# Which expert pairs return their rows through DRAM, and when those rows are read back

## The chip, the cores and the metric

The kernel runs on one core of a Trainium2 chip. The metric is the device time of one launch in microseconds. Its TensorE (PE) does matrix products, VectorE (DVE), ScalarE (ACT) and GpSimd (POOL) do the rest, and SyncE (SP) issues most of the transfers. All engines run their own instruction streams and wait for one another on semaphores.

## What is computed

Two layers of a decoder step over 288 tokens (256 of a new sequence and 8 x 4 of running ones), width 1024. A layer mixes (RG-LRU, a convolution group, retention) and then applies a mixture of experts; this case is about the second half:

```python
g_sel = argmax(softmax(x @ wg + bg))                 # one of 4 groups
top_v, top_i = top_k(logits of that group, 2)         # 2 of its 8 experts
gates = p_group * softmax(top_v)
for e in range(32):                                   # every expert
    h = silu(x @ w1[e]) * (x @ w3[e])                 # 1024 -> 256
    y += gates[:, e] * (h @ w2[e])                    # 256 -> 1024
x = x + y
```

The kernel gathers for each expert the tokens that chose it (up to 64 slots), so 288 x 2 = 576 of the 2048 slots hold a token.

## The kernel before

The 32 experts of a layer are worked off in 16 pairs, two experts of 64 slots each making 128 rows. Their weights stream from DRAM: w1, w3 and w2 of an expert are 1 MB each, and a ring in SBUF holds four experts. SP issues w1 and w3 of an expert when the products of the expert four before it have been made (it waits on bank "h"), and w2 when the products of an earlier pair's w2 are done (bank "y1"). The weights of two experts stay outside the ring: expert 6 (EARLY, in pair 3) and expert 16 (SPARE, in pair 8), whose w1 and w3 lie in `uT` and `mixT`. SP's queue is one list of transfers, in the order in which the weights are used.

For each pair PE does `up` for the even expert (32 matmuls with w1 and w3, line 1135), `down` for the pair before (16 matmuls with w2, line 1158), the transposes of hidden rows and of the next pair's tokens, and `up` for the odd expert. ACT copies each `up` out of PSUM (lines 2201, 2223, one copy for each expert), scales the results of `down` by the gates into `ysb` (`results`, line 2196), and does the tanh. DVE does the gating product (`hidden`) and the evacuation of the tokens. POOL gathers the rows of pair g + 3 by an indirect DMA.

The results of a pair, 128 rows in slot order, go back to the tokens in one of two ways:

- **By DRAM**, pairs 0 to 5 (`VIA_DRAM = 6`): POOL scatters `ysb` to `y_scratch` (`scatter`, line 2344). ACT may write the next `ysb` when the scatter has landed. Later `read_back` (line 2363) fetches for each token of a tile of 128, 128 or 32 tokens its one or two rows (two indirect DMAs), into two buffers `again[0]` and `again[1]` that `clear` has set to zero, and DVE adds both to `x` (`sums`, line 1919). The three tiles share the two buffers, so this happens in three rounds: POOL reads tile 1 at pair 6, tile 2 at pair 9, tile 0 at pair 11, and DVE adds at pairs 9, 11 and 13 (`READ_BACK`).
- **By matmul**, pairs 6 to 15: POOL makes a 0/1 matrix from the token numbers (`way_back`, line 2353), DVE splits `ysb` into three bf16 parts (`rest`, `low`), and PE multiplies (`give_back`, lines 1172, 1181, 1187). Parts 0 and 1 of pair p come at the end of pair p + 1, parts 2, 3 and 4 after the even `up` of pair p + 2. DVE adds the five banks to `x` (`given_back`).

PE's list for one pair of the second kind is:

```python
up(2 * pair, it)
if p - 2 >= VIA_DRAM:
    give_back(p - 2, (2, 3))
    give_back(p - 2, (4,))
down(1 - pair, it if pair else it - 1)
...
up(2 * pair + 1, it)
...
if p - 1 >= VIA_DRAM:
    give_back(p - 1, (0, 1))
```

Of the kernel before, what the change touches and what calls it, by code (L numbers as in the profile page):

```python
# [46 lines left out]
NPAIR = NE // 2  # L47
VIA_DRAM = 6
BY_MATMUL = NPAIR - VIA_DRAM
READ_BACK = {VIA_DRAM + 3: 1, VIA_DRAM + 5: 2, VIA_DRAM + 7: 0}  # L50

# [112 lines left out]
def x1_turn(pair):  # L164

    return pair + max(0, pair - VIA_DRAM - 2)


def back_plan():

    plan = {}
    for p in range(VIA_DRAM, NPAIR):
        for a, b in enumerate((6, 7, 6, 7, 1) if p < NPAIR - 2 else (6, 7, 0, 1, 6) if p < NPAIR - 1 else (3, 7, 0, 1, 2)):
            plan[p, a] = b, x1_turn(p + 3) - 1 if p < NPAIR - 2 and a == 4 else PER_BANK[b] - EXPERT_BASE[b]
            PER_BANK[b] += 1
    return plan
# [25 lines left out]
def build(nc, ins, outs):  # L202
# [11 lines left out]
    with ExitStack() as ctx:  # L214
# [132 lines left out]


        again = [ttf, sgf[:, 512:512 + D]]
        assert used <= 512  # L350
        spare_w1 = uT[:, 0:2048].rearrange("p (k f) -> p k f", k=KT)
        spare_w3 = mixT[:, :, :].rearrange("p k t -> p (k t)")[:, 0:2048].rearrange("p (k f) -> p k f", k=KT)
        spare_w2 = [a[:, :, :].rearrange("p a n -> p (a n)")[:, 0:D] for a in (qT, kr)]

        glsf = gls[:, :, :, :].rearrange("p c b t -> p (c b t)")
# [365 lines left out]
        def _(pe):  # L721
# [54 lines left out]
            for l in range(DEPTH):  # L776
# [385 lines left out]
                def give_back(p, parts):  # L1162

                    pair, it = pair_of(p)
                    turn_ = l * BY_MATMUL + p - VIA_DRAM
                    if 0 in parts:
                        pe.wait_ge(back_ready, turn_ + 1)
                    if 4 in parts:
                        b = begin("back4", pair, it)
                        for n_, y in enumerate((y_top, y_mid, y_low)):  # L1170
                            for q in range(4):
                                i = pe.matmul(b[32 * q:32 * q + 32, 0:256], back[:, pair, SEQ:NT], y[:, 256 * q:256 * q + 256],  # L1172
                                              start=n_ == 0, stop=n_ == 2, skip_group_check=True)
                        finish(i, "back4", pair, it)
                        return
                    banks = []
                    for a in parts:
# [12 lines left out]

                def give_back_last():

                    pe.wait_ge(back_ready, BY_MATMUL * (l + 1))
                    for a in range(4):
# [20 lines left out]
                def experts2_back(p):  # L1215

                    pair, it = pair_of(p)
                    up(2 * pair, it)
                    if p - 2 >= VIA_DRAM:
                        give_back(p - 2, (2, 3))  # L1220
                        give_back(p - 2, (4,))
# [5 lines left out]
                    if p + 1 < NPAIR:  # L1227
                        tokens(pair + 1, it, (1,))
                        turn_h(2 * pair + 1, it)
                    if p - 1 >= VIA_DRAM:  # L1230
                        give_back(p - 1, (0, 1))
# [10 lines left out]
                experts2(1, 0)  # L1242
                for it in range(1, VIA_DRAM // 2):
                    experts2(0, it)
                    experts2(1, it)
                for p in range(VIA_DRAM, NPAIR):
                    experts2_back(p)
# [53 lines left out]
        def _(dve):  # L1301
# [87 lines left out]
            for l in range(DEPTH):  # L1389
# [425 lines left out]
                def overs():  # L1815

                    do(dve.tensor_copy(r_if[:, :, :], r_idx[:, :, 0:2]))
                    own(S(again_here[:, :, :], r_if[:, :, :], float(2 * VIA_DRAM), None, ALU.is_lt))
                    do(S(again_rank[:, :, :], rank[:, :, :], float(SLOTS), None, ALU.is_lt))
# [71 lines left out]
                def rest(p, j):  # L1891

                    pair, it = pair_of(p)
                    if j == 0 and p > VIA_DRAM:
                        xfull(dve, "back4", *pair_of(p - 1), l)
                    xfreed(dve, f"y{j}", pair, it, l)
                    T(y_rest[:, halves[j]], ysb[:, halves[j]], y_top[:, halves[j]], ALU.subtract).then_inc(rest_ready, 1)  # L1897

                def low(p):
                    turn_ = l * (BY_MATMUL - 1) + p - VIA_DRAM  # L1900
                    for j, s in enumerate(halves):
# [3 lines left out]
                def clear():  # L1905

                    own(dve.memset(again[0], 0.0))
                    own(dve.memset(again[1], 0.0))
                    own.wait()
                    dve.sem_inc(again_clear, 1)  # L1910

                def sums(p, t):
# [5 lines left out]
                    for k in range(2):  # L1918
                        T(x[0:n, t, :], x[0:n, t, :], again[k][0:n, :], ALU.add).then_inc(sums_added, 1)
                        dve.wait_ge(sums_added, 6 * l + 2 * list(READ_BACK).index(p) + k + 1)  # L1920

# [21 lines left out]
                def experts2_back(p):  # L1943
                    pair, it = pair_of(p)
                    if p - 2 >= VIA_DRAM:
                        given_back(p - 2, (0, 1))
                        if p in READ_BACK:
                            sums(p, READ_BACK[p])
                        given_back(p - 2, (2, 3, 4))
                    if p - 1 >= VIA_DRAM:  # L1950
                        rest(p - 1, 0)
                    hidden(2 * pair, it)
                    if p - 1 >= VIA_DRAM:
                        rest(p - 1, 1)
                        low(p - 1)
                    if p + 1 < NPAIR:
                        tokens(pair + 1, it)
                    hidden(2 * pair + 1, it)
                    if p in READ_BACK and p + 2 in READ_BACK:
                        clear()  # L1960

# [6 lines left out]
                experts2(1, 0)  # L1968
                with dve.Fori(1, VIA_DRAM // 2) as it:
                    experts2(0, it)  # L1970
                    experts2(1, it)
                clear()
                for p in range(VIA_DRAM, NPAIR):
                    experts2_back(p)
# [49 lines left out]
        def _(act):  # L2024
# [27 lines left out]
            for l in range(DEPTH):  # L2052
# [145 lines left out]
                def one(u, it, first=False):  # L2198
# [3 lines left out]
                    if u % 2 == 0 and not first:  # L2202
                        before = (1 - u // 2, it if u else it - 1)

                        act.wait_ge(scattered, 16 * (l * VIA_DRAM + 2 * before[1] + before[0]))
                        results(*before)
# [10 lines left out]
                def one_back(p, i):  # L2217
# [6 lines left out]
                    if i == 0:  # L2224
                        xfull(act, "back4", *pair_of(p - 2), l)
                        results(*pair_of(p - 1))
# [13 lines left out]
                one(3, 0)  # L2240
                with act.Fori(1, VIA_DRAM // 2 + 1) as it:
                    for u in range(4):
                        one(u, it)
                for p in range(VIA_DRAM + 2, NPAIR):
                    for i in range(2):
                        one_back(p, i)
# [25 lines left out]
        def _(pool):  # L2272
# [3 lines left out]
            for l in range(DEPTH):  # L2276
# [71 lines left out]
                def way_back(g):  # L2348

                    if g - 2 >= VIA_DRAM:  # L2350
                        xfull(pool, "back4", *pair_of(g - 2), l)
                    for t, (o, n) in enumerate(TILES):
# [3 lines left out]
                def read_back(t):  # L2356

                    o, n = TILES[t]
                    pool.wait_ge(again_ready, l + 1)
                    pool.wait_ge(scattered, 16 * VIA_DRAM * (l + 1))  # L2360
                    pool.wait_ge(again_clear, 3 * l + list(READ_BACK.values()).index(t) + 1)
                    for k in range(2):
                        pool.indirect_dma_start(out=again[k][0:n, :], out_offset=None, in_=y_dram,
                                                in_offset=bass.IndirectOffsetOnAxis(ap=again_at[0:n, t, k:k + 1], axis=0),
# [9 lines left out]
                for g in range(NPAIR):  # L2374
                    if g + 3 < NPAIR:
                        gather(g + 3)
                    if g < VIA_DRAM:
                        scatter(g)
                    else:
                        way_back(g)  # L2380
                    if g in (VIA_DRAM + 3, VIA_DRAM + 5):
                        read_back(READ_BACK[g + 2])
                    if g + 2 < NPAIR:
                        if g >= VIA_DRAM:
# [3 lines left out]
                    if g == VIA_DRAM:  # L2388
                        read_back(READ_BACK[g + 3])
                o = O[l]  # L2390
# [36 lines left out]
```

## Time and profile before

| | |
|---|---|
| time, median of 3 runs | 856.33 us (855.98 to 857.28) |
| the profiled execution, its own time | 856.64 us |
| its span | 854.8 us |
| PE busy | 817.4 us, 96% of the span |
| DVE / ACT / POOL busy | 480.7 / 176.1 / 145.6 us |
| moved from and to DRAM | 260.12 MB, mean 304 GB/s |
| pairs 0 to 15 of layer 0 / of layer 1 on PE | about 184 to 429 us / 605 to 846 us |

Times in the profile are microseconds from the span's start. The profiled execution takes 1.8 us more than its span. The page gives shares over the whole span; the expert part has to be read from windows and from the order in time.

### The profile page before, as it was taken

What the parts mean: (1) busy time and instruction counts of PE and PEld (TensorE: products, weight loads), DVE (VectorE), ACT (ScalarE), POOL (GpSimd) and SP (SyncE); (2) the same over time, 40 slices, a digit from 0 to 9 for tenths busy, and PEclk for the clock granted to TensorE, in tenths of its full rate; (3) what the DMA queues carried; (4) which work ended last, traced back from release to release, by engine and by line L of the source; (5) the groups of instructions that cost most, each with busy time, mean ns of one, the idle gap of its engine ahead of it and who ended that gap; (6) DMA issues with size and microseconds to landing.
All of it is one profiled execution on the core that took longest, in us unless ns stands there. A gap on an engine that the chain in (4) does not pass through costs nothing.

```text
span 854.8 us, 13483 instructions
## 1 busy us (share of the span) xinstructions
PE 817.4 (96%) x5250; PEld 462.8 (54%) x5250; DVE 480.7 (56%) x1097; ACT 176.1 (21%) x361; POOL 145.6 (17%) x197
## 2 busy tenths in 40 slices
PE   7999999999997899999999999999999979999995
PEld 5664554675654555555466545447655545545552
DVE  3497787372212377775555977955521215777666
ACT  3213122302121111111221221232022111111113
POOL 0030031011211322321000300300211112412220
PEclk9999999999999999999999999999999999999998
DMA  9942962779999999999960339357799999999961
GB/s 320 318 156 104 375 208 74 274 257 405 417 414 382 413 415 403 415 414 400 374 247 0 148 138 257 102 140 268 307 411 414 416 413 417 413 401 415 414 257 57
DMA packets 89946, 260.12 MB, mean 304 GB/s; under 512 B 30424, under 2 KB 40044, under 8 KB 73946
## 3 DMA queue, kind: packets, MB, share of 16 engines
q1 hardware_dynamic: 80410, 247.01, 75.5%
q0 software_dynamic: 7680, 9.39, 3.2%
q10 hardware_dynamic: 1792, 2.84, 0.9%
q8 instruction: 44, 0.72, 0.4%
q14 instruction: 20, 0.16, 0.1%
HBM read 265.22 MB, written 15.18 MB: 328 GB/s over the span
## 4 chain that ended last, share of the span: by engine, by line
PE 89%; DVE 4%; issue 3%; DMA 2%; SPq 1%; ACT 1%; DVEq 0%; POOLq 0%; ACTq 0%
PE psum L1135 27%; PE psum L1158 13%; PE psum L793 12%; PE psum L733 8%; PE psum L802 7%; PE psum L991 5%; PE psum L1187 4%; PE psum L1181 2%; PE psum L812 2%; DMA ring<-in_w_in 1%; PE psum L1032 1%; PE psum L1172 1%; PE psum L868 1%; PE psum L1022 1%; PE psum L893 1%
## 5 line engine op out<-in xcount | busy, mean ns | idle before, releaser
L1135 PE MATMUL psum<-ring,arena 128*64 128x256 f32 x1920 | 222.1, 384 | 9.2 <-issue 8.0
L1135 PEld LDWEIGHTS psum<-ring,arena 128*64 128x64 f32 x1920 | 138.3, 138 | 78.7 <-issue 19.1
L1158 PE MATMUL psum<-ring,arena 128*64 128x512 f32 x480 | 116.4, 597 | 7.6 <-issue 7.6
L793 PE MATMUL psum<-ring,uT 128*128 128x512 f32 x256 | 113.6, 596 | 0.5 <-DVE uT L1369 0.4
L1877 DVE TENSOR_TENSOR arena<-psum,gff 128x512 f32<-128x512 f32 x64 | 43.6, 687 | 69.3 <-PE psum L733 69.3
L1885 DVE SCALAR_TENSOR_TENSOR arena<-arena,psum 128x128 f32<-128x128 f32 x64 | 18.3, 285 | 108.4 <-ACT arena L2215 94.8
L793 PEld LDWEIGHTS psum<-ring,uT 128*128 128x128 f32 x256 | 47.6, 190 | 55.1 <-issue 53.2
L1931 DVE TENSOR_TENSOR x<-x,psum 128x512 f32<-128x512 f32 x80 | 51.4, 683 | 40.9 <-PE psum L1187 35.3
L2196 ACT ACTIVATE arena<-psum,sg 128x512 f32<-128x512 f32 x64 | 44.0, 687 | 121.9 <-PE psum L1158 120.1
L1158 PEld LDWEIGHTS psum<-ring,arena 128*64 128x64 f32 x480 | 35.3, 137 | 61.2 <-issue 60.1
L2331 POOL DMA_INDIRECT rows<-xn_scratch,sg x32 | 33.5, 1047 | 204.1 <-PE psum L733 119.2
L802 PE MATMUL psum<-uT,ring 128*128 128x288 f32 x256 | 63.8, 407 | 0.7 <-DMA ring<-in_w_in 0.7
L1456 DVE SCALAR_TENSOR_TENSOR cb<-glp,prm,cb 128x256 f32<-128x256 f32 x120 | 57.3, 546 | 0.6 <-DVE hst L1608 0.4
L991 PE MATMUL psum<-ring,mixT 128*128 128x512 f32 x128 | 57.2, 597 | 0.0
L802 PEld LDWEIGHTS psum<-uT,ring 128*128 128x128 f32 x256 | 48.1, 190 | 14.7 <-DMA ring<-in_w_in 1.2
L733 PE MATMUL psum<-const,rows 128*128 128x128 f32 (+1 forms) x304 | 48.7, 289 | 0.5 <-DMA rows<-xn_scratch,sg 0.3
L733 PEld LDWEIGHTS psum<-const,rows 128*128 128x128 f32 (+1 forms) x304 | 39.5, 193 | 14.7 <-issue 12.8
L2353 POOL TENSOR_SCALAR kT<-const,sg 128x128 bf16<-128x128 f32 (+3 forms) x60 | 41.8, 711 | 17.8 <-PE psum L1172 17.2
L1897 DVE TENSOR_TENSOR v<-arena 128x512 f32<-128x512 f32 x36 | 24.8, 688 | 27.6 <-ACT arena L2196 27.6
L2201 ACT ACTIVATE arena<-psum 128x256 f32<-128x256 f32 x30 | 11.5, 383 | 136.9 <-PE psum L1135 136.9
L2223 ACT ACTIVATE arena<-psum 128x256 f32<-128x256 f32 x32 | 12.3, 383 | 129.9 <-PE psum L1135 129.9
L991 PEld LDWEIGHTS psum<-ring,mixT 128*128 128x128 f32 x128 | 23.7, 190 | 27.0 <-issue 26.6
(330 smaller groups left out, 938.1 us busy)
## 6 DMA issues: line engine op xcount, KB each, us to landing
ring<-in_moe_w SPq DMA_DIRECT2D x180, 1024.0 KB, 19.2
ring<-in_w_in SPq DMA_DIRECT2D x24, 1024.0 KB, 14.0
ring<-in_w_out SPq DMA_DIRECT2D x8, 1024.0 KB, 7.2
y_scratch<-in_w_out SPq DMA_DIRECT2D x1, 2304.0 KB, 17.9
arena<-in_state_ret SPq DMA_DIRECT2D x16, 128.0 KB, 5.6
out<-arena SPq DMA_DIRECT2D x16, 128.0 KB, 2.5
xn_scratch<-rows ACTq DMA_DIRECT2D x4, 512.0 KB, 4.0
mixT<-in_moe_w SPq DMA_DIRECT2D x2, 1024.0 KB, 4.9
```

What stands on the lines that cost most here:

```text
L733: return pe.transpose(out, in_, ident[0:n, 0:n])
L793: i = pe.matmul(b, uTk[:, k, 128 * t:128 * t + 128], w[:, k, :], start=k == 0, stop=k == KT - 1)
L802: i = pe.matmul(b, w[:, k, 128 * (c % 4):128 * (c % 4) + 128], uTk[:, k, :], start=k == 0, stop=k == KT - 1)
L991: i = pe.matmul(b, mixT[:, k, 128 * t:128 * t + 128], w[:, :, k, :], start=k == 0, stop=k == 3, skip_group_check=True)
L1135: i = pe.matmul(b[64 * j:64 * j + 64, 0:FE], xsT[:, u // 2, k, s], weight13(e, j, k), start=k == 0, stop=k == KT - 1, skip_group_check=True)
L1158: i = pe.matmul(b[64 * q:64 * q + 64, :], hT[:, q, f, :], weight2(4 * it + 2 * pair + q, f, j), start=f == 0, stop=f == 1, skip_group_chec ...
L1187: i = pe.matmul(b, back[:, pair, 64 * (a - a % 2):64 * (a - a % 2) + 128], y[:, 512 * (a % 2):512 * (a % 2) + 512], start=False, stop=y is ...
L1456: chain[c] = own(STT(dst, glp[:, c, k:k + SEQ], w, dst, ALU.mult, ALU.add))
L1877: T(xsT[:, g2 % 2, k0:k0 + 4, :], psum[:, b, :].rearrange("p (k s) -> p k s", k=4), g3[:, k0:k0 + 4, :], ALU.mult).then_inc(bank_free[b], 1)
L1931: i = T(s, s, psum[:, b, :], ALU.add)
L2196: A(ysb[:, 512 * j:512 * j + 512], psum[:, b, :], ACT.Copy, scale=gate_col[:, pair:pair + 1]).then_inc(bank_free[b], 1)
L2353: i = pool.tensor_scalar(back[:, g % 2, o:o + n] if g < NPAIR - 1 else back_last[:, o:o + n], C("iota")[:, 0:n], tok[:, t, g:g + 1], None, ...
```

## The change

Pairs 0 to 3 and 8 and 9 go by DRAM, pairs 4 to 7 and 10 to 15 by matmul: six and ten as before. The three tiles have two buffers each (`mixT` for tile 0, the old two for tile 1, `uT` for tile 2), all cleared at once ahead of pair 10; POOL issues the six read-backs one after the other after pair 11, and DVE adds at pairs 13 (tile 1), 14 (tile 2) and 15 (tile 0). The test of which expert numbers go by DRAM has two more DVE operations in each layer. The loops of the first pairs are shorter, and pairs 4 and 5 are written out with the rest.

```diff
-VIA_DRAM = 6
-BY_MATMUL = NPAIR - VIA_DRAM
-READ_BACK = {VIA_DRAM + 3: 1, VIA_DRAM + 5: 2, VIA_DRAM + 7: 0}
+
+FIRST = 4
+VIA_DRAM = (*range(FIRST), 8, 9)
+BY_MATMUL = [p for p in range(NPAIR) if p not in VIA_DRAM]
+READ_BACK = {13: 1, 14: 2, 15: 0}
...
-    return pair + max(0, pair - VIA_DRAM - 2)
+    return pair + sum(p <= min(pair, NPAIR) - 3 for p in BY_MATMUL)
...
-        again = [ttf, sgf[:, 512:512 + D]]
...
+        mixTf = mixT[:, :, :].rearrange("p k t -> p (k t)")
+        again = [[mixTf[:, 0:D], mixTf[:, D:2 * D]], [ttf, sgf[:, 512:512 + D]], [uT[:, 0:D], uT[:, D:2 * D]]]
...
-                    if p - 2 >= VIA_DRAM:
+                    if p - 2 in BY_MATMUL:
                         give_back(p - 2, (2, 3))
                         give_back(p - 2, (4,))
...
-                    if p - 1 >= VIA_DRAM:
+                    if p - 1 in BY_MATMUL:
                         give_back(p - 1, (0, 1))
...
-                    own(S(again_here[:, :, :], r_if[:, :, :], float(2 * VIA_DRAM), None, ALU.is_lt))
+
+                    lo, hi = 2 * VIA_DRAM[FIRST], 2 * VIA_DRAM[-1] + 1
+                    do(S(again_here[:, :, :], r_if[:, :, :], float(lo), None, ALU.is_ge))
+                    do(STT(again_here[:, :, :], r_if[:, :, :], float(hi), again_here[:, :, :], ALU.is_le, ALU.mult))
+                    do(STT(again_here[:, :, :], r_if[:, :, :], float(2 * FIRST), again_here[:, :, :], ALU.is_lt, ALU.add))
...
-                    own(dve.memset(again[0], 0.0))
-                    own(dve.memset(again[1], 0.0))
+                    for t, (_, n) in enumerate(TILES):
+                        for k in range(2):
+                            own(dve.memset(again[t][k][0:n, :], 0.0))
...
-                clear()
-                for p in range(VIA_DRAM, NPAIR):
+                for p in range(FIRST, NPAIR):
+                    if p == VIA_DRAM[-1] + 1:
+                        clear()
                     experts2_back(p)
...
                     if i == 0:
-                        xfull(act, "back4", *pair_of(p - 2), l)
+                        if p - 2 in VIA_DRAM:
+                            act.wait_ge(scattered, 16 * (l * len(VIA_DRAM) + VIA_DRAM.index(p - 2) + 1))
+                        else:
+                            xfull(act, "back4", *pair_of(p - 2), l)
                         results(*pair_of(p - 1))
...
-                    if g < VIA_DRAM:
+                    if g in VIA_DRAM:
                         scatter(g)
                     else:
                         way_back(g)
-                    if g in (VIA_DRAM + 3, VIA_DRAM + 5):
-                        read_back(READ_BACK[g + 2])
+                    if g == VIA_DRAM[-1] + 2:
+                        for t in READ_BACK.values():
+                            read_back(t)
```

## Rows read from the trace of the kernel before

**Rows 1.** The page, the span in 40 slices of 21.4 us: DMA share, rate.

```profile
DMA  9942962779999999999960339357799999999961
GB/s 320 318 156 104 375 208 74 274 257 405 417 414 382 413 415 403 415 414 400 374 247 0 148 138 257 102 140 268 307 411 414 416 413 417 413 401 415 414 257 57
```

**Rows 2.** Busy time by windows: PE, PEld, DVE, ACT, POOL, clock, DMA share, GB/s.

```profile
206.00:222.00 16.00, 16.00 (x126) 9.37 (x124) 3.57 (x9) 3.25 (x8) 3.31 (x4) 1.00 1.02 417
...
270.00:286.00 16.00, 13.04 (x86) 8.28 (x86) 1.57 (x4) 1.73 (x4) 3.12 (x6) 0.89 1.03 411
...
366.00:382.00 16.00, 16.00 (x120) 8.41 (x120) 11.46 (x20) 2.83 (x7) 3.48 (x5) 1.00 1.02 414
```

**Rows 3.** Timeline of ACT: start and length of each copy of an `up`.

```profile
210.91 0.38 ACT L2201 ACTIVATE arena<-psum 128x256 f32<-128x256 f32 x1 [3.28 <-PE psum L1135]
218.75 0.38 ACT L2201 ACTIVATE arena<-psum 128x256 f32<-128x256 f32 x1 [3.56 <-PE psum L1135]
223.28 0.38 ACT L2201 ACTIVATE arena<-psum 128x256 f32<-128x256 f32 x1 [3.34 <-PE psum L1135]
...
262.38 0.38 ACT L2201 ACTIVATE arena<-psum 128x256 f32<-128x256 f32 x1 [3.34 <-PE psum L1135]
276.08 0.38 ACT L2201 ACTIVATE arena<-psum 128x256 f32<-128x256 f32 x1 [7.43 <-PE psum L1135]
...
297.50 0.38 ACT L2223 ACTIVATE arena<-psum 128x256 f32<-128x256 f32 x1 [4.67 <-PE psum L1135]
...
313.25 0.38 ACT L2223 ACTIVATE arena<-psum 128x256 f32<-128x256 f32 x1 [4.61 <-PE psum L1135]
323.14 0.38 ACT L2223 ACTIVATE arena<-psum 128x256 f32<-128x256 f32 x1 [3.55 <-PE psum L1135]
329.00 0.38 ACT L2223 ACTIVATE arena<-psum 128x256 f32<-128x256 f32 x1 [4.61 <-PE psum L1135]
...
631.30 0.38 ACT L2201 ACTIVATE arena<-psum 128x256 f32<-128x256 f32 x1 [3.28 <-PE psum L1135]
...
714.85 0.38 ACT L2223 ACTIVATE arena<-psum 128x256 f32<-128x256 f32 x1 [4.67 <-PE psum L1135]
```

**Rows 4.** Timeline of PE, pairs 6 and 7 of layer 0: start, length, idle before.

```profile
270.68 5.36 PE L1135 MATMUL psum<-ring,arena 128*64 128x256 f32 x32 [2.12 <-issue]
...
277.61 3.67 PE L1135 MATMUL psum<-ring,arena 128*64 128x256 f32 x32 [0.65 <-issue]
282.90 3.65 PE L1158 MATMUL psum<-ring,arena 128*64 128x512 f32 x16 [1.62 <-issue]
...
287.92 3.67 PE L1135 MATMUL psum<-ring,arena 128*64 128x256 f32 x32 [0.56 <-issue]
```

**Rows 5.** Timeline: issue of w3 of expert 27, and its `up`, both layers.

```profile
355.01 0.43 SPq L540 DMA_DIRECT2D ring<-in_moe_w  x1
...
382.42 3.67 PE L1135 MATMUL psum<-ring,arena 128*64 128x256 f32 x32
...
772.37 0.79 SPq L540 DMA_DIRECT2D ring<-in_moe_w  x1
...
799.78 3.67 PE L1135 MATMUL psum<-ring,arena 128*64 128x256 f32 x32
```

**Rows 6.** DMA view, issues at 355.01, 772.37: KB, us to landing.

```profile
ring<-in_moe_w SPq DMA_DIRECT2D x1, 1024.0 KB, 23.2
...
ring<-in_moe_w SPq DMA_DIRECT2D x1, 1024.0 KB, 21.4
```

**Rows 7.** Groups of instructions: clears, additions, scatters, read-backs; busy, mean ns.

```profile
L1907 DVE MEMSET tt<- 128x1024 f32 x6 | 5.5, 912 | 1.0 <-issue 1.0
...
L1919 DVE TENSOR_TENSOR x<-x,tt 128x1024 f32<-128x1024 f32 x4 | 5.0, 1260 | 0.4
...
L2344 POOL DMA_INDIRECT y_scratch<-arena,sg x12 | 12.2, 1013 | 92.1 <-ACT arena L2196 68.0 <-issue 24.1
...
L2363 POOL DMA_INDIRECT tt<-y_scratch,sg x6 | 6.9, 1158 | 5.0 <-DVEq L1910 3.7 <-issue 1.3
```

More of the change, by code:

```diff
@@ L164, in x1_turn @@
 def x1_turn(pair):
-    return pair + max(0, pair - VIA_DRAM - 2)
+    return pair + sum(p <= min(pair, NPAIR) - 3 for p in BY_MATMUL)
 def back_plan():
     plan = {}
-    for p in range(VIA_DRAM, NPAIR):
+    for p in BY_MATMUL:
         for a, b in enumerate((6, 7, 6, 7, 1) if p < NPAIR - 2 else (6, 7, 0, 1, 6) if p < NPAIR - 1 else (3, 7, 0, 1, 2)):
@@ L1164, in give_back @@
                     pair, it = pair_of(p)
-                    turn_ = l * BY_MATMUL + p - VIA_DRAM
+                    turn_ = l * len(BY_MATMUL) + BY_MATMUL.index(p)
                     if 0 in parts:
@@ L1191, in give_back_last @@
                 def give_back_last():
-                    pe.wait_ge(back_ready, BY_MATMUL * (l + 1))
+                    pe.wait_ge(back_ready, len(BY_MATMUL) * (l + 1))
                     for a in range(4):
@@ L1242, in _ @@
                 experts2(1, 0)
-                for it in range(1, VIA_DRAM // 2):
+                for it in range(1, FIRST // 2):
                     experts2(0, it)
                     experts2(1, it)
-                for p in range(VIA_DRAM, NPAIR):
+                for p in range(FIRST, NPAIR):
                     experts2_back(p)
@@ L1893, in rest @@
                     pair, it = pair_of(p)
-                    if j == 0 and p > VIA_DRAM:
-                        xfull(dve, "back4", *pair_of(p - 1), l)
+                    if j == 0 and p > BY_MATMUL[0]:
+                        xfull(dve, "back4", *pair_of(BY_MATMUL[BY_MATMUL.index(p) - 1]), l)
                     xfreed(dve, f"y{j}", pair, it, l)
@@ L1899, in low @@
                 def low(p):
-                    turn_ = l * (BY_MATMUL - 1) + p - VIA_DRAM
+                    turn_ = l * (len(BY_MATMUL) - 1) + BY_MATMUL.index(p)
                     for j, s in enumerate(halves):
@@ L1918, in sums @@
                     for k in range(2):
-                        T(x[0:n, t, :], x[0:n, t, :], again[k][0:n, :], ALU.add).then_inc(sums_added, 1)
+                        T(x[0:n, t, :], x[0:n, t, :], again[t][k][0:n, :], ALU.add).then_inc(sums_added, 1)
                         dve.wait_ge(sums_added, 6 * l + 2 * list(READ_BACK).index(p) + k + 1)
@@ L1944, in experts2_back @@
                     pair, it = pair_of(p)
-                    if p - 2 >= VIA_DRAM:
+                    if p - 2 in BY_MATMUL:
                         given_back(p - 2, (0, 1))
@@ L1949, in experts2_back @@
                         given_back(p - 2, (2, 3, 4))
-                    if p - 1 >= VIA_DRAM:
+                    if p - 1 in BY_MATMUL:
                         rest(p - 1, 0)
                     hidden(2 * pair, it)
-                    if p - 1 >= VIA_DRAM:
+                    if p - 1 in BY_MATMUL:
                         rest(p - 1, 1)
@@ L1958, in experts2_back @@
                     hidden(2 * pair + 1, it)
-                    if p in READ_BACK and p + 2 in READ_BACK:
-                        clear()
                 dve.wait_ge(st_out, 128 * (l + 1))
@@ L1968, in _ @@
                 experts2(1, 0)
-                with dve.Fori(1, VIA_DRAM // 2) as it:
+                with dve.Fori(1, FIRST // 2) as it:
                     experts2(0, it)
                     experts2(1, it)
-                clear()
-                for p in range(VIA_DRAM, NPAIR):
+                for p in range(FIRST, NPAIR):
+                    if p == VIA_DRAM[-1] + 1:
+                        clear()
                     experts2_back(p)
@@ L2203, in one @@
                         before = (1 - u // 2, it if u else it - 1)
-                        act.wait_ge(scattered, 16 * (l * VIA_DRAM + 2 * before[1] + before[0]))
+                        act.wait_ge(scattered, 16 * (l * len(VIA_DRAM) + 2 * before[1] + before[0]))
                         results(*before)
@@ L2240, in _ @@
                 one(3, 0)
-                with act.Fori(1, VIA_DRAM // 2 + 1) as it:
+                with act.Fori(1, FIRST // 2) as it:
                     for u in range(4):
                         one(u, it)
-                for p in range(VIA_DRAM + 2, NPAIR):
+                for p in range(FIRST, NPAIR):
                     for i in range(2):
@@ L2348, in way_back @@
                 def way_back(g):
-                    if g - 2 >= VIA_DRAM:
-                        xfull(pool, "back4", *pair_of(g - 2), l)
+                    before = [p for p in BY_MATMUL if p < g and p % 2 == g % 2]
+                    if before:
+                        xfull(pool, "back4", *pair_of(before[-1]), l)
                     for t, (o, n) in enumerate(TILES):
@@ L2359, in read_back @@
                     pool.wait_ge(again_ready, l + 1)
-                    pool.wait_ge(scattered, 16 * VIA_DRAM * (l + 1))
-                    pool.wait_ge(again_clear, 3 * l + list(READ_BACK.values()).index(t) + 1)
+                    pool.wait_ge(scattered, 16 * len(VIA_DRAM) * (l + 1))
+                    pool.wait_ge(again_clear, l + 1)
                     for k in range(2):
-                        pool.indirect_dma_start(out=again[k][0:n, :], out_offset=None, in_=y_dram,
+                        pool.indirect_dma_start(out=again[t][k][0:n, :], out_offset=None, in_=y_dram,
                                                 in_offset=bass.IndirectOffsetOnAxis(ap=again_at[0:n, t, k:k + 1], axis=0),
@@ L2380, in _ @@
                         way_back(g)
-                    if g in (VIA_DRAM + 3, VIA_DRAM + 5):
-                        read_back(READ_BACK[g + 2])
+                    if g == VIA_DRAM[-1] + 2:
+                        for t in READ_BACK.values():
+                            read_back(t)
                     if g + 2 < NPAIR:
-                        if g >= VIA_DRAM:
+                        if g in BY_MATMUL:
                             for j in range(2):
```

2 lines of the change are left out of this document (removed).

## The prediction

> **What bounds the kernel now.** The page comes first: PE is busy for 96% of the span, but its DMA rows [rows 1] show a second resource that is full in just the part that the change touches. In slices 9 to 19 and 29 to 37, the expert parts of both layers, the DMA share is 9 tenths or more and the rate sits between 374 and 417 GB/s. The windows [rows 2] say the same at full share, 1.02 and 1.03, with 411 to 417 GB/s both where PE has no gap (206 to 222, 366 to 382) and where it has (270 to 286: 13.04 us busy of 16). So the transfers never rest, and PE rests where weights have not come.
>
> Next come the copies that ACT makes of each `up` [rows 3]; they are a clock of the pairs. Without give-back a pair goes from one even copy to the next in 223.28 - 210.91 = 12.37 us, split 7.84 (even to odd) and 4.53 (odd to even). With give-back it takes 329.00 - 313.25 = 15.75 us, split 9.89 and 5.86. One give-back therefore costs PE 3.38 us: 2.05 (parts 2, 3, 4) and 1.33 (parts 0, 1). A pair's weights are 6 transfers of 1 MiB, 6.29 MB; at 414 GB/s they need 15.2 us, and the gathers share the rate. So at 12.37 us a pair PE outruns the transfers, and at 15.75 us the two are about level.
>
> That makes the stalls. From pair 2 to pair 8 layer 0 takes 297.50 - 210.91 = 86.59 us, where PE's own work is 6 x 12.37 + 1.33 = 75.55: 11.0 us of stalls. Layer 1 takes 714.85 - 631.30 = 83.55, so 8.0 us. They lie in pairs 4, 6 and 7. The timeline of PE [rows 4] shows four of them as idle time put down to issue, each ending when a weight tile lands; and in the first `up` 32 matmuls took 5.36 us for the usual 3.67, in the window whose granted clock is 0.89 [rows 2]. That is 1.7 us for the lower of the two levels (1.2 GHz) behind 2.1 us of idling. From pair 8 on PE has no gap. This is the room in which the change works: 19 us of stalls in pairs 4 to 7, against give-back work further on that is on PE's path in full.
>
> **The change, part by part.** *Pairs 4 and 5 get give-backs on PE.* Two whole ones, 6.76 us a layer, are executed from the end of pair 5 to the middle of pair 7, where PE idles now. I step through layer 0. Pair 5 is unchanged. The even copy of pair 6 comes 1.33 later than 262.38, at 263.7. PE's own work would put the odd copy at 263.7 + 9.89 = 273.6, but the weights let the `up` start only at 270.68 [rows 4]; at full clock it ends 3.67 later, at 274.35 (now 276.08). Then 5.86 more would be 280.2, but the weights of pair 7 allow 277.61 + 3.67 = 281.3, as now. Pair 7's odd `up`: PE's own work gives 281.3 + 9.89 = 291.2; the weights give 287.92 + 3.67 = 291.6, as now. So the even copy of pair 8 stays at 297.5. In layer 1, stepped the same way, PE's own work and the weights also come out within 0.8 us of each other at each step, and the even copy of pair 8 stays at 714.8. The new work costs nothing because it lies in waits for weights; with that cover gone it would cost its 6.76 us.
>
> *Pairs 8 and 9 lose theirs.* PE leaves out 1.33 + 3.38 + 2.05 = 6.76 us between the end of pair 9 and the middle of pair 11, a stretch in which it has no gap. There PE moves ahead by the whole amount, if the weights are there. The transfers are already at full share, so earlier issues don't make them land earlier; I take the landings as fixed and ask how long each expert's last tile has been there when its `up` starts. The least in layer 0 is expert 27: issued at 355.01, landed 23.2 later [rows 5, 6] at 378.2, used at 382.42, which leaves 4.2 us. In layer 1: 772.37 + 21.4 = 793.8, used at 799.78, 6.0 us. All later experts leave more. So of the 6.76 us the layers keep 4.2 and 6.0; the rest turns into short waits in pairs 12 and 13.
>
> *What the transfers have to move.* The same six scatters and six read-backs, shifted. All of both are issued before expert 27 lands, before and after, so their sum ahead of this tile is the same. Two scatters less stand ahead of pair 7's weights: less than 1 us earlier, which PE's own work (291.2 against 291.6) would hardly use.
>
> *DVE.* The clears were 3 x 2 of 912 ns in three places [rows 7] and are now 6 in a row, 5.5 us, ahead of pair 10. After `hidden` of pair 9 DVE is next wanted when PE has done an `up` and a `down` (3.67 + 3.65), about 8 us after the odd copy with the transposes, so 1 to 2 us are to spare. `sums` adds 2 x 1.26 us [rows 7] at pairs 13, 14 and 15 instead of 9, 11 and 13; DVE is busy for 11.5 of 16 us in the window that holds pair 13's [rows 2], and PE has no gap there. At pair 15 they fall between `given_back` parts 0, 1 and parts 2, 3, 4, for which PE still has an `up` to do. The two more small operations lie behind the first `up` of pair 0, before DVE idles. Nothing, each; if the cover of the clears failed, the cost is bounded by 5.5 us a layer.
>
> *POOL and ACT.* POOL issues six read-backs of about 1.16 us in a row [rows 7], 7 us, with the gate of pair 13 and the gather of pair 15 behind them in its queue. Both are wanted a whole pair later, at least 12 us. The results of pair 9 wait for the scatter of pair 8, which now stands in a run of short pairs just as the scatters of pairs 0 to 5 do. Nothing, bounded by some 2 us each.
>
> **Sum.** 856.64 (the profiled execution's own time) - 4.2 - 6.0 = 846.4. It stands 0.3 above the median of the runs, so 846.1 us.
>
> **The Trainium skill.** The page "DMA: Bandwidth & Descriptors", section "Where 436 GB/s comes from", gives 435 GB/s as the ceiling of the fabric into SBUF. By that a pair's weights would need 14.5 us, less than PE's 15.75, and no wait would come back; the rows show 414. The same section says that for DRAM to SBUF the memory side binds at about 358 GB/s; by that a pair would need 17.6 us and PE would be waiting everywhere. The rows show neither.
>
> **Rivals.**
>
> *The whole 13.5 us is kept* (856.6 - 13.5 = 843.1). It needs landings of experts 24 to 31 that are 2.6 us earlier in layer 0 and 0.8 in layer 1. For it: 4.2 is the time of one tile that took 23.2 us, and fewer scatters stand early. Against: full DMA share in every window.
>
> *The landings slip* (848 to 852). The six read-backs in one round, and the scatters of 8 and 9, compete with weights when there is no reserve left. Each 1 us of slip of expert 27 or later costs 1 us in its layer; By the share of pairs, 6/16 of 576 rows of 4 KB come back, 0.88 MB or 2.1 us at 414 GB/s in each layer; 1 to 3 us a layer is what I allow.
>
> *Hidden anyway* (855 to 857, no change). If the transfers alone set the end of the layer, moving PE work moves nothing. This is what the page's 358 GB/s would mean. Against it stand the 4.2 and 6.0 us that PE is behind the landings.
>
> *Slower: the clock* (from 857.5 up). PE now waits shortly and often in pairs 12 to 15. If the clock falls at such waits as it did at 270.68, each `up` behind one costs 1.7 us. The 16 `up`s of these pairs in both layers would cost 27 us, so 873; the change loses from seven on. The skill's page "TensorE: Matmul & The Clock Gate", section "HAM oscillation — how this bites in real kernels", describes waits for DMA between bursts of matmuls that throttle the clock again and again. Against: of the four waits of [rows 4] only one was followed by a long `up`, and the new waits are well under 2 us.
>
> **How the numbers follow.** My forecast (845 to 848) has 0.57, the whole gain 0.15, slipping landings 0.17, no change 0.05, slower 0.06. The range takes in the whole gain and most of the slip: 842.5 to 851. Within 0.2% (1.7 us, about what a measurement of this kernel can tell) 0.05; faster 0.89; slower 0.06.
>
> **What would show it.** In the changed kernel the even copy of pair 8 should stand within 1 us of its old distance from pair 2's (86.6 and 83.6 us), with give-back matmuls where the idle was. Pairs 9 to 11 should take 14.4, 12.4 and 13.7 us or so between even copies. Waits of PE put down to issue should appear in pairs 12 and 13, with `up`s that start as tiles land. DMA should be at full share and the last expert tile should land at the same distance from pair 0. I am wrong if pair 8 comes later than now (cover in pairs 5 to 7 too small), if pair 10 or 11 waits for DVE or ACT (the clears, the scatter), or if an `up` takes 5 us.

## The result, and the profile after

The changed kernel takes 849.3 us (4 runs, 848.73 to 850.46) against 856.8 us for the kernel before (4 runs, 855.98 to 857.82): ratio 0.991, 95% interval 0.9893 to 0.9928. Two later sets of runs gave 0.9904 (0.9878 to 0.993) and 0.9909 (0.9894 to 0.9924). So it is 7.5 us faster (8.1 and 8.2 in the later sets), where 10.2 us had been forecast. The measured 849.3 us lies above the forecast's 845 to 848, in the band that was given to slipping landings, and inside the stated range of 842.5 to 851.

The page of the profiled execution (848.73 us), span and slices, answering to [rows 1]:

```profile
span 846.9 us, 13378 instructions
...
PEclk9999999999999999999999999999999999999998
DMA  9942972869999999999990329347799999999981
GB/s 313 317 164 107 377 201 79 274 236 412 414 414 373 416 414 414 413 398 413 357 335 2 149 99 294 108 90 282 292 410 416 414 414 417 415 414 395 416 329 62
```

The transfers are as full as before in both expert parts. The timeline of ACT, the copies of the `up`s (line 2230 is the old 2223), answering to [rows 3]:

```profile
210.47 0.38 ACT L2208 ACTIVATE arena<-psum 128x256 f32<-128x256 f32 x1 [3.28 <-PE psum L1138]
...
263.91 0.38 ACT L2230 ACTIVATE arena<-psum 128x256 f32<-128x256 f32 x1 [4.61 <-PE psum L1138]
274.32 0.38 ACT L2230 ACTIVATE arena<-psum 128x256 f32<-128x256 f32 x1 [4.07 <-PE psum L1138]
280.62 0.38 ACT L2230 ACTIVATE arena<-psum 128x256 f32<-128x256 f32 x1 [5.05 <-PE psum L1138]
290.92 0.38 ACT L2230 ACTIVATE arena<-psum 128x256 f32<-128x256 f32 x1 [3.96 <-PE psum L1138]
296.78 0.38 ACT L2230 ACTIVATE arena<-psum 128x256 f32<-128x256 f32 x1 [4.61 <-PE psum L1138]
...
312.53 0.38 ACT L2230 ACTIVATE arena<-psum 128x256 f32<-128x256 f32 x1 [4.61 <-PE psum L1138]
...
326.94 0.38 ACT L2230 ACTIVATE arena<-psum 128x256 f32<-128x256 f32 x1 [3.28 <-PE psum L1138]
...
339.31 0.38 ACT L2230 ACTIVATE arena<-psum 128x256 f32<-128x256 f32 x1 [3.28 <-PE psum L1138]
...
353.09 0.38 ACT L2230 ACTIVATE arena<-psum 128x256 f32<-128x256 f32 x1 [4.61 <-PE psum L1138]
...
370.03 0.38 ACT L2230 ACTIVATE arena<-psum 128x256 f32<-128x256 f32 x1 [5.00 <-PE psum L1138]
...
389.05 0.38 ACT L2230 ACTIVATE arena<-psum 128x256 f32<-128x256 f32 x1 [4.61 <-PE psum L1138]
...
628.59 0.38 ACT L2208 ACTIVATE arena<-psum 128x256 f32<-128x256 f32 x1 [3.28 <-PE psum L1138]
...
711.03 0.38 ACT L2230 ACTIVATE arena<-psum 128x256 f32<-128x256 f32 x1 [4.61 <-PE psum L1138]
```

The even copies of pairs 9 to 14 stand 14.41, 12.37, 13.78, 16.94 and 19.02 us apart. The first three are the short pairs that were forecast; the last two are longer than PE's own 15.75, by 1.2 and 3.3 us. (A pair's time is counted here from its even copy to the next pair's.) In layer 0 the even copy of pair 2 to that of pair 8 takes 86.31 us (before 86.59), in layer 1 82.44 (before 83.55).

The time between the two profiled executions adds up as follows, E2 being the even copy of pair 2 and O15 the odd copy of pair 15:

| stretch | before | after | difference |
|---|---|---|---|
| start to E2, layer 0 | 210.91 | 210.47 | -0.44 |
| E2 to O15, layer 0 | 206.28 | 203.79 | -2.49 |
| O15 to E2 of layer 1 | 214.11 | 214.33 | +0.22 |
| E2 to O15, layer 1 | 203.25 | 198.05 | -5.20 |
| O15 to the end of the span | 20.25 | 20.26 | +0.01 |

The timeline of PE, the products with idle time put down to issue, pairs 12 and 13 of layer 0:

```profile
360.07 3.67 PE L1138 MATMUL psum<-ring,arena 128*64 128x256 f32 x32 [0.76 <-issue]
...
366.32 3.67 PE L1138 MATMUL psum<-ring,arena 128*64 128x256 f32 x32 [0.33 <-issue]
...
373.21 3.65 PE L1161 MATMUL psum<-ring,arena 128*64 128x512 f32 x16 [1.33 <-issue]
...
379.48 3.67 PE L1138 MATMUL psum<-ring,arena 128*64 128x256 f32 x32 [1.79 <-issue]
```

These four are PE's only waits of more than 0.25 us in the two pairs. The last line is the `up` of expert 27. The issue of its w3 in the timeline of SP, answering to [rows 5]:

```profile
350.80 1.50 SPq L543 DMA_DIRECT2D ring<-in_moe_w  x1
```

and the same issue in the DMA view (KB, us to landing), answering to [rows 6]:

```profile
ring<-in_moe_w SPq DMA_DIRECT2D x1, 1024.0 KB, 28.6
```

It lands at 350.8 + 28.6 = 379.4 and PE starts at 379.48: the wait is for this tile, as forecast. But measured from E2 it lands at 168.9, in the kernel before at 378.2 - 210.91 = 167.3: 1.6 us later, where equal had been assumed. In layer 1 the same tile is 0.7 us later (issued at 762.70, 29.1 us to landing, 163.2 from E2; before 162.5). It was issued earlier than before, at 140.3 us from E2 against 144.1, and still did not land earlier.

One execution is not enough for the 1.6 us. The changed kernel was profiled twice more, in the two later sets. The same `up` of expert 27 in layer 0 there, also straight behind a wait, so that its start stands for the landing:

```profile
379.64 3.67 PE L1139 MATMUL psum<-ring,arena 128*64 128x256 f32 x32 [0.52 <-issue]
```

```profile
378.44 3.67 PE L1139 MATMUL psum<-ring,arena 128*64 128x256 f32 x32 [0.50 <-issue]
```

| changed kernel | E2, layer 0 | `up` of expert 27 from E2, layer 0 / 1 | E2 to O15, layer 0 / 1 | less than before |
|---|---|---|---|---|
| first profile | 210.47 | 169.0 / 163.3 | 203.79 / 198.05 | 2.5 + 5.2 |
| second set | 211.96 | 167.7 / 163.1 | 202.45 / 197.90 | 3.8 + 5.35 |
| third set | 211.03 | 167.4 / 163.1 | 202.19 / 197.90 | 4.1 + 5.35 |

So in layer 0 the tile is 0.1 to 0.4 us late in two profiles and 1.6 in one; in layer 1 it is 0.6 to 0.7 us late in all three. The kernel before has one profile.

### The profile page after: what moved, and what is told of

The parts are those of the page before. It is cut to its first block, busy times and chain, and to the rows that moved or that the text cites. A ratio compares the mean times of both kernels' runs of the same rounds, so it can differ in the third digit from the quotient of the medians.

```text
span 846.9 us, 13378 instructions
## 1 busy us (share of the span) xinstructions
PE 815.5 (96%) x5250; PEld 464.3 (55%) x5250; DVE 481.4 (57%) x1101; ACT 176.2 (21%) x361; POOL 140.9 (17%) x197
## 2 busy tenths in 40 slices
DMA packets 89947, 259.64 MB, mean 307 GB/s; under 512 B 30541, under 2 KB 40161, under 8 KB 73947
## 4 chain that ended last, share of the span: by engine, by line
PE 90%; DVE 4%; issue 2%; SPq 2%; DMA 1%; ACT 1%; DVEq 0%; POOLq 0%; ACTq 0%
PE psum L1138 27%; PE psum L1161 13%; PE psum L796 12%; PE psum L736 8%; PE psum L805 7%; PE psum L994 5%; PE psum L1190 4%; PE psum L1184 2%; PE psum L815 2%; PE psum L1035 1%; PE psum L1175 1%; DMA ring<-in_w_in 1%; PE psum L871 1%; PE psum L1025 1%; SPq L531 1%
## 5 line engine op out<-in xcount | busy, mean ns | idle before, releaser
L2230 ACT ACTIVATE arena<-psum 128x256 f32<-128x256 f32 x48 | 18.4, 383 | 192.4 <-PE psum L1138 192.4
L2364 POOL TENSOR_SCALAR kT<-const,sg 128x128 bf16<-128x128 f32 (+3 forms) x60 | 36.7, 626 | 17.8 <-PE psum L1175 17.2
L1943 DVE TENSOR_TENSOR x<-x,psum 32x256 f32<-32x256 f32 x80 | 33.0, 413 | 0.8
## 6 DMA issues: line engine op xcount, KB each, us to landing
y_scratch<-in_w_out SPq DMA_DIRECT2D x1, 2304.0 KB, 18.8
```

The source lines that it names most:

```text
L2364: i = pool.tensor_scalar(back[:, g % 2, o:o + n] if g < NPAIR - 1 else back_last[:, o:o + n], C("iota")[:, 0:n], tok[:, t, g:g + 1], None, ...
```

## The experiments

Each kernel was timed beside runs of the kernel before in the same set. Experiments 1 to 4 are one set, 5 to 7 the second, 8 and 9 the third; all are forms of the changed kernel.

**1. The early half alone.**

```diff
-VIA_DRAM = (*range(FIRST), 8, 9)
+VIA_DRAM = (*range(FIRST),)
...
-                    if p == VIA_DRAM[-1] + 1:
+                    if p == 10:
...
-                    if g == VIA_DRAM[-1] + 2:
+                    if g == 11:
```

> Only pairs 0 to 3 go by DRAM; pairs 4 to 15, so 8 and 9 too, go by matmul: the half of the change that moves pairs 4 and 5, without the half that relieves pairs 8 and 9. Theory (weights' landings set the pace to pair 8, PE from there): the give-backs of 4 and 5 lie in waits for weights and cost nothing, from pair 8 on PE has the work that it had in the kernel before. So the time of the kernel before, 856.8, or up to 2 us less, since four scatters and a third of the rows read back have gone from the transfers: 855 to 857. Rival (give-back work is on PE's path wherever it stands): two give-backs of 3.38 us more than the kernel before in each layer, 856.8 + 13.5 = 870.

Measured: 866.6 us, ratio 1.0104 (1.007 to 1.0138), a miss for both. From pair 8 on every pair but pair 10 took 15.75 us, as the theory says; pair 10 itself took 22.19 us in layer 0 and 21.93 in layer 1. (From the even copy of pair 2 to that of pair 8 this execution took 84.1 and 83.9 us, in layer 0 2.5 less than the kernel before.) The timeline there, DVE and PE:

```profile
324.76 0.91 DVE L1913 MEMSET mixT<- 128x1024 f32 x1 [0.16 <-issue]
...
330.12 0.91 DVE L1913 MEMSET uT<- 32x1024 f32 x1 [0.16 <-issue]
331.19 1.29 DVE L1936 TENSOR_TENSOR x<-x,psum 128x512 f32<-128x512 f32 x2 [0.16 <-DVE uT L1913]
331.93 1.21 PE L1184 MATMUL psum<-arena,kT 128*128 128x512 bf16 x2 [3.42 <-DVE x L1936]
...
335.54 4.89 PE L1161 MATMUL psum<-ring,arena 128*64 128x512 f32 x16
```

The six clears keep DVE for 6.3 us. Pair 8 has a give-back here, whose first banks DVE must add to `x` before PE gets them for the next parts; PE waits 3.42 us, and its next products run at the lower level (16 of line 1161 in 4.89 us for 3.65). The windows of the same stretch, granted clock third from the end:

```profile
324.00:332.00 8.00, 4.58 (x38) 2.47 (x35) 6.85 (x11) 0.38 (x1) 2.63 (x4) 0.95 1.02 410
332.00:341.00 9.00, 9.00 (x40) 2.87 (x40) 4.20 (x8) 1.21 (x2) 0.00 (x0) 0.66 0.98 404
```

In the changed kernel itself the same clears are just covered (timeline of DVE): the last ends at 330.73, and the next `hidden` had to wait 0.52 us more for ACT.

```profile
324.46 0.91 DVE L1916 MEMSET mixT<- 128x1024 f32 x1 [0.16 <-issue]
...
329.82 0.91 DVE L1916 MEMSET uT<- 32x1024 f32 x1 [0.16 <-issue]
331.26 0.29 DVE L1892 SCALAR_TENSOR_TENSOR arena<-arena,psum 128x128 f32<-128x128 f32 x1 [0.52 <-ACT arena L2222]
```

**2. The late half alone.**

```diff
-FIRST = 4
+FIRST = 6
```

> Pairs 0 to 5, 8 and 9 go by DRAM: the half of the change that relieves pairs 8 and 9 of give-back, without the half that gives it to pairs 4 and 5. Theory (landings): to pair 8 nothing changes, after it PE moves ahead until it meets the landings, as in the changed kernel, 849.3; two scatters and a third of the rows more stand among the transfers in each layer, about 0.7 us of rate each, and that now costs: 849.5 to 852. Rival (PE's work sets the time): 13.5 us of PE work less than the changed kernel, 836.

Measured: 852.1 us, ratio 0.9935 (0.9914 to 0.9957). 27 us of give-back less than in experiment 1's form, and 13.5 less than in the changed kernel, yet no faster than the latter: by the ratios it is 2 us behind, with intervals that overlap. From E2 to O15 its profile takes 203.46 and 200.15 us. The theory holds; the time by the ratio, 0.9935 x 856.8 = 851.2, is in its range, the median just above.

**3. Eight pairs by DRAM.**

```diff
-VIA_DRAM = (*range(FIRST), 8, 9)
+VIA_DRAM = (*range(FIRST), 6, 7, 8, 9)
```

> Pairs 0 to 3 and 6 to 9 go by DRAM, eight instead of six, so PE has two give-backs less than in the changed kernel in each layer, here in pairs 7 to 9 where it has no reserve of weights yet. Theory (landings): no gain, 849.5 to 852, because the landings of the experts after pair 11 are later, if anything. Rival (PE's work sets the time): 849.3 - 13.5 = 836.

Measured: 855.9 us, ratio 0.997 (0.995 to 0.999): no gain over the changed kernel but a loss of about 5 us by the ratios, where 0.2 to 2.7 had been expected. So PE's work does not set the time here either. Pair 8 comes sooner (E2 to the even copy of pair 8 in 84.9 and 81.2 us), but from there to O15 it takes 119.8 and 121.0 us, against 117.5 and 115.6 in the changed kernel's first profile: pairs 10 to 13 take 16.6 to 18.8 us each. The `up` of expert 27 starts at 170.0 and 167.4 us from E2, later than in any profile of the changed kernel. The page says that 261.31 MB were moved for 259.64; that is 4.0 us at 414 GB/s, an estimate of the part that the bytes have. In pair 10 PE waits 2.52 us (2.62 in layer 1) and its next 16 matmuls take 5.11 us (5.28) for 3.65:

```profile
327.76 5.11 PE L1161 MATMUL psum<-ring,arena 128*64 128x512 f32 x16 [2.52 <-issue]
```

PE waits for weights again in the pairs behind it, so this lower clock does not have to show in the time. The start to E2, where the kernels are alike, takes 210.2 to 214.8 us in all profiles, and this execution has the 214.8, so part of its profiled time, perhaps of its median, lies there.

**4. Three rounds of read-backs.**

```diff
-                    if g == VIA_DRAM[-1] + 2:
-                        for t in READ_BACK.values():
-                            read_back(t)
+                    if g + 2 in READ_BACK:
+                        read_back(READ_BACK[g + 2])
```

> The changed kernel with its six read-backs issued two after pair 11, two after pair 12 and two after pair 13 instead of all after pair 11; the buffers and the additions are the same. In the changed kernel the last tile of expert 27 lands 1.6 us (layer 0) and 0.7 us (layer 1) later than in the kernel before, beside the shift of its start, and the DMA rate is down to some 285 to 390 GB/s for several us after the round. Theory (the round in one takes from the rate and stands ahead of expert 27, where PE has no reserve): most of it moves behind expert 27, 0.7 to 1.2 us less in each layer, 847 to 848.3. Rival (the number of rows counts, not where they are read): 849.3.

Measured: 848.25 us, ratio 0.9899 (0.9869 to 0.9928). By time alone not parted from the changed kernel. From E2 to O15 its trace takes 201.76 and 197.32 us; against the changed kernel's three profiles that is 0.4 to 2.0 us less in layer 0 and 0.6 to 0.7 in layer 1. See 8.

The second set took the changed kernel itself along (849.5 us, ratio 0.9904).

> The changed kernel itself once more, timed on the same chip as the three others of this set. All theories: its ratio to the kernel before as first measured, 0.989 to 0.993.

**5. Fewer bytes for one expert.**

```diff
+                n = 256 if e == 22 else 2048
-                sp.dma_start(ring[:, 3 * u, :], w1[l, e].rearrange("(p k) f -> p (k f)", p=128)).then_inc(granule_in[3 * u], 16)
+                sp.dma_start(ring[:, 3 * u, 0:n], w1[l, e].rearrange("(p k) f -> p (k f)", p=128)[:, 0:n]).then_inc(granule_in[3 * u], 16)
```

The same is done to its w3. Its w2 is loaded whole, against the words of the expectation: so 1.84 MB less in each layer, 4.4 us at 414 GB/s.

> The changed kernel with only an eighth of the weights of expert 22 loaded in each layer (the rest of its place in the ring keeps the weights of expert 18, so its products are others); 2.75 MB less in each layer, 6.6 us at 414 GB/s. PE's work is the same. Theory (what is missing of the 13.5 us is the lateness of weights behind pair 11, 4.3 us in layer 0 and 1.6 in layer 1): all later tiles land some 6 us earlier, the waits in pairs 11 to 13 vanish, 5 to 6 us less than the changed kernel. Rival (the waits there come from something else, DVE, ACT or POOL): no difference to the changed kernel.

Measured: 843.2 us, ratio 0.9822 (0.9796 to 0.9848), 6.35 us below the changed kernel beside it. From the even copy of pair 8 to O15 it takes 112.96 and 112.94 us. That is 119.7 - 6.76 = 112.94, the whole of the left-out give-backs and not a wait more. From E2 to O15 the two layers take 3.7 and 1.8 us less than in the changed kernel's profile of this set, 5.5 in all, as expected; the rest of the 6.35 is not in these stretches.

**6. The early half again, clears in twos.**

```diff
-                    if p == 10:
-                        clear()
...
+                    if p in (8, 9, 10):
+                        clear(p - 8)
```

`clear` takes one tile here, and gives its signal after the third.

> As the run with only pairs 0 to 3 by DRAM, but the six clears in twos at the ends of pairs 8, 9 and 10 instead of all six ahead of pair 10. There pair 10 took 22.2 and 21.9 us for 15.75: PE waited 3.4 us for DVE to free a bank and then ran its next products at the lower clock. Theory (the row of clears is the whole difference from the kernel before, the give-backs of pairs 4 and 5 cost nothing): 6.4 us less in each layer, so 12 to 13 us less than the first form, a ratio of 0.995 to 1.000 to the kernel before. Rival (two more give-backs are on PE's path and the clears only hit pair 10 by chance of place): at most 4 us less than the first form.

Measured: 856.5 us, ratio 0.9981 (0.9965 to 0.9997), 10 us below experiment 1 by the medians of two sets; pair 10 takes 15.75 us in both layers, and the even copy of pair 8 to O15 119.68 and 119.71 us, as in the kernel before (119.69 and 119.70). Two more give-backs in each layer than the kernel before has cost nothing. The ratio is in the range expected; the 12 to 13 us below the first form are not reached, although pair 10 gives back 6.4 and 6.2 us, because the first form's profile was 2.0 us shorter ahead of pair 8 in layer 0.

**7. No read-backs.** The `read_back` and `sums` calls are left out, the wait for the scatters stays:

```diff
-                        for t in READ_BACK.values():
-                            read_back(t)
+                        pool.wait_ge(scattered, 16 * len(VIA_DRAM) * (l + 1))
...
-                        if p in READ_BACK:
-                            sums(p, READ_BACK[p])
```

> The changed kernel without the six read-backs and their additions, so that the rows of the pairs that went by DRAM are missing in x. Theory (the read-backs ahead of expert 27 make its tile late): expert 27 lands 3 us earlier or so, and of the waits of 5.6 us (layer 0) and 2 us (layer 1) behind pair 11 some 3 and 1.5 us go: 3.5 to 5 us less than the changed kernel. Rival (the rate is set by the weights alone, the read-backs take little): under 1 us less.

Measured: 844.6 us, ratio 0.983 (0.9803 to 0.9856), 4.9 us below the changed kernel; from E2 to O15 2.9 and 1.7 us less than its profile of this set. By the pages 257.57 MB were moved for 259.64: the read-backs are 1.03 MB a layer, 2.5 us at 414 GB/s. Busy time by windows (the last columns are granted clock, DMA share and GB/s), first the changed kernel's first profile, then this one:

```profile
356.00:372.00 16.00, 14.80 (x112) 8.53 (x108) 10.46 (x19) 2.58 (x6) 6.15 (x8) 1.00 1.03 389
372.00:388.00 16.00, 12.99 (x92) 7.68 (x94) 9.73 (x19) 2.20 (x5) 2.81 (x4) 1.00 1.02 417
```

```profile
356.00:372.00 16.00, 15.73 (x117) 8.59 (x116) 8.94 (x18) 2.58 (x6) 2.82 (x5) 1.00 1.02 416
372.00:388.00 16.00, 16.00 (x119) 8.25 (x117) 9.05 (x18) 2.58 (x6) 2.80 (x4) 1.00 1.02 415
```

PE's idle time in pairs 12 and 13 has all but gone, and the rate is back from 389 to 416 GB/s. The windows stand 2.4 us apart in distance from E2; at the same distances (148 to 164 and 164 to 180 us) the changed kernel of this set has PE busy for 13.61 and 15.48 us at 390 and 416 GB/s, this one for 15.73 and 16.00 at 415 and 417.

**8. Three rounds beside the changed kernel**, which took 849.0 us here, ratio 0.9909 (0.9894 to 0.9924).

> The changed kernel, as the measure for the two others of this set on the same chip: 0.989 to 0.993 of the kernel before.

> The three rounds of read-backs once more, now on the same chip as the changed kernel. In the first run its trace was shorter by 2.0 us in layer 0 and 0.7 in layer 1 from the even copy of pair 2 to the odd copy of pair 15, while the medians of two sets did not part them. Theory (the round in one costs waits behind pair 11): 1.5 to 3 us less than the changed kernel. Rival: the same.

Measured: 845.6 us, ratio 0.9869 (0.9852 to 0.9887), 3.4 us below the changed kernel, somewhat more than expected. Between the two profiles of this set 0.7 and 0.8 us lie from E2 to O15 in the layers and 0.75 ahead of E2, where the kernels are alike. So the traces show 1.5 us of the gain in the layers; the rest of the 3.4 is not shown to come from the rounds. The `up` of expert 27 starts at 166.2 and 162.2 us from E2, for 167.4 and 163.1. The windows:

```profile
356.00:372.00 16.00, 15.13 (x115) 8.39 (x114) 10.81 (x19) 2.59 (x6) 6.14 (x7) 1.00 1.02 413
372.00:388.00 16.00, 15.09 (x115) 8.33 (x114) 10.83 (x20) 2.59 (x6) 4.91 (x6) 1.00 1.02 400
```

From 148 to 180 us behind E2 PE is busy for 30.2 us, in the changed kernel of this set for 28.9. The dip of the rate comes a window later, when tile 0 is read behind pair 13. In this set the three rounds are faster than both kernels; in the first set the same form (experiment 4) was not parted from the changed kernel.

**9. The router's weights later, on top of 8.**

```diff
                         load_states(sp, l + 1)
-                        load_router(sp, l + 1)
...
                         for g in gs:
                             project_in(l + 1, g)
+                    load_router(sp, l + 1)
```

> The three rounds, and the next layer's router weights (144 KB in short pieces, loaded in pair 6 of layer 0 while PE waits for weights) loaded behind the next layer's first projection weights instead. Theory (the transfers set layer 0's time and short pieces take more of it than their bytes: the rate falls to 373 to 382 GB/s in their slice): 1 to 2.5 us less than the three rounds alone, layer 0 only. Rival (their place does not matter, or the layer after waits for them): the same or slower.

Measured: 845.4 us, ratio 0.9867 (0.9847 to 0.9886), so the same as 8; the rival holds. In window 256 to 272 the rate is 365 GB/s with the later load and 372 without. So the dip there is not the router's weights.

## Why the prediction was right, and where it was off

*Transfers full, PE waiting.* Right. Experiments 2, 3, 5 and 7 say it four times: less PE work does not help (852.1, 855.9), fewer bytes do (843.2, 844.6), and 5 and 7 have the matmuls of the changed kernel. Experiment 7 leaves out work of DVE and POOL too, but experiment 5 keeps it and loses the waits all the same.

*Give-backs of pairs 4 and 5 in the waits.* Right. The even and odd copies of pairs 6 and 7 were forecast at 263.7, 274.35, 281.3 and 291.6, that of pair 8 at 297.5; they stand at 263.91, 274.32, 280.62, 290.92 and 296.78, with a start earlier by 0.44. Experiment 6 does this half alone and takes what the kernel before takes, or a little less. In layer 1 pair 8 came 1.1 us sooner than forecast (82.4 us from pair 2's copy in all three profiles, where 83.55 was to stay within 1 us). PE's own work with the give-backs is 6 x 12.37 + 1.33 + 6.76 = 82.31, so it hardly waited there: the weights were there earlier than "as now".

*Pairs 8 and 9.* The 6.76 us are left out exactly: experiment 5 gets all of them in both layers. Pairs 9 to 11 took 14.41, 12.37 and 13.78 us for the 14.4, 12.4 and 13.7 forecast, so the scatter of pair 8 and POOL's row of read-backs held up nothing there.

*Landings fixed; the layers keep 4.2 and 6.0.* This is the term that was mis-sized. For 10.2 us the layers kept 7.7 in the first profile (and 0.2 was lost between them), 9.2 and 9.4 in the two others. The tile that ends the run of PE is the one named, expert 27. It was held fixed and landed 0.6 to 0.7 us later in layer 1, and 0.1, 0.4 and 1.6 us later in layer 0; 6.0 - 0.7 = 5.3 and 4.2 - 1.6 = 2.6 are what the first profile kept. Of what layer 1 kept, 1.1 us came ahead of pair 8 and only 4.1 to 4.2 behind it, where all 6.0 had been put.

The reason given for fixed landings was that the same read-backs stand ahead of this tile before and after. What they cost can be seen: the 0.88 MB a layer that the prediction took by the share of pairs are 1.03 MB, and while they stand in one round the rate is 389 to 391 GB/s over 16 us, where the lowest window of the kernel before between pair 8 and this tile has 397 to 398. Without them (experiment 7) the two layers are 4.6 us shorter, and spread over three rounds (experiments 4 and 8) 1.0 to 1.8 us shorter than in the changed kernel's two later profiles. So the sum ahead of the tile being the same nearly held the landing, and moving part of it behind the tile was the gain that the forecast did not see. By time the result stands in the band of the slipping landings; the slip itself was 0.1 to 1.6 us a layer, where that rival allowed 1 to 3.

*DVE.* Right that the clears are covered, by 0.5 us rather than by 1 to 2, and the bound for failed cover was too low: 5.5 us a layer were allowed, and in experiment 1 it is 22.19 - 15.75 = 6.4, with the lower clock behind the wait. `sums` at pairs 13 to 15 cost nothing: in experiment 5, which has them, those pairs take 15.75 us.

*The clock.* The rival did not come: in the changed kernel each of the four waits of 0.3 to 1.8 us in pairs 12 and 13 of layer 0 is followed by products of the usual 3.67 or 3.65 us. It did come in experiment 1, behind a wait of 3.42 us, and in experiment 3, behind 2.52 and 2.62.

*What stays open.* In layer 0 the last tile of expert 31 lands 201.5 us from E2 in the first profile and at 200.6 and 200.7 in the two others, against 199.8 before. A lower rate in one window of 16 us, 389 for 413, is worth 0.9 us, which is what the two others show. Why both tiles were about 1 us later still in the first profile is not shown: at the same distance from E2 its rate is 391 GB/s and that of the second 390. The median gain of 7.5 to 8.2 us is also less than what the layers kept in the later profiles, perhaps because the start to E2 differs by up to 4.6 us between executions of kernels that are alike there; what makes it differ is not shown. The loss of experiment 3 beyond its bytes is not traced.

## What to carry to other kernels

Work moved into the waits of a busy engine cost nothing here (experiment 6), but what it frees elsewhere is only kept as far as the weights have landed ahead. So list, for each transfer, landing against first use, and take the smallest distance behind the place that gets faster. Once that reserve is spent, what stands just ahead of the tightest tile counts: here the read-backs were 5.0 us of bytes at 414 GB/s over both layers, and leaving them out gained 4.6 us in the traces and 4.9 by the medians. Spread such transfers, or put them behind that tile. When buffers are made separate and their clearing is gathered in one place, ask what the engine owes in that very place; here the cover is 0.5 us. And a difference of 1 us in one trace needs a second trace of the same kernel before it is given a cause.

## What the runs showed of the hardware that was not expected

With a round of six indirect reads in flight beside the stream of weights, the whole rate was 389 GB/s over 16 us at full DMA share; without them it was 416 in the same window (experiment 7).

The length of one wait did not decide what the clock did. A granted clock of 0.66 over 9 us followed a wait of PE of 3.42 us (experiment 1), and waits of up to 1.8 us in the changed kernel left the matmuls' length as it was. In between both happened. In the kernel before, the `up` behind 2.12 us took 5.36 us. In experiment 2 the same `up` of pair 6 in layer 0 and the one after it kept the usual length behind 2.14 and 2.36 us, and the window 270 to 286 has a granted clock of 1.00:

```profile
272.20 3.67 PE L1138 MATMUL psum<-ring,arena 128*64 128x256 f32 x32 [2.14 <-issue]
...
279.14 3.67 PE L1138 MATMUL psum<-ring,arena 128*64 128x256 f32 x32 [2.36 <-issue]
```
